# Block 2 of a fused two-block kernel: the transposing turns of the normalised tiles go one tile later, and both first token halves follow the last turn

## The reference, cut to what matters

```python
for l in range(2):
    h = rmsnorm(x, mix_norm_g[l])
    x = x + mixing_layer(h, ...)          # h @ w_in, ..., y @ w_out
    h = rmsnorm(x, ffn_norm_g[l])
    x = x + (silu(h @ w_gate) * (h @ w_up)) @ w_down
return rmsnorm(x, final_norm_g)
```

## Time and profile before

| | |
|---|---|
| time, median of 3 runs | 2886.91 us (2886.65 to 2887.95) |
| time of the profiled execution | 2892.95 us |
| its span | 2891.0 us |
| TensorE matmuls busy | 2699.0 us, 93% |
| TensorE weight loads busy | 2014.6 us, 70% |
| DVE busy | 1096.4 us, 38% |
| ACT busy | 829.0 us, 29% |
| POOL busy | 697.6 us, 24% |
| mean granted TensorE clock | 0.976 |

### The profile page before, as it was taken

How to read it: one execution, slowest core, us unless ns; L and a number is a source line. 1 busy time by engine, 2 the same in 40 slices (tenths; PEclk the granted TensorE clock), 3 DMA queues, 4 the chain that set the end, 5 groups by cost and what they waited for, 6 DMA issues and landing times.

```text
span 2891.0 us, 35167 instructions
## 1 busy us (share of the span) xinstructions
PE 2699.0 (93%) x14496; PEld 2014.6 (70%) x14496; DVE 1096.4 (38%) x1800; ACT 829.0 (29%) x1444; POOL 697.6 (24%) x297
## 2 busy tenths in 40 slices
PE   7999999999989996999999799999999998999998
PEld 4777777786447885444444397888878896988877
DVE  3555555533341124112121488420014697300034
ACT  2433333333333222000000224532222327322122
POOL 2222222220013410000000032233434332343433
PEclk8999999999999997999999999999999999999999
DMA  7111111102012323899999721123222221223221
GB/s 256 52 58 58 58 58 58 36 30 80 27 39 78 127 92 131 351 409 409 409 408 409 293 84 63 59 73 102 88 96 94 73 88 44 74 89 101 89 100 44
DMA packets 212563, 382.38 MB, mean 132 GB/s; under 512 B 10833, under 2 KB 145877, under 8 KB 211413
## 3 DMA queue, kind: packets, MB, share of 16 engines
q1 hardware_dynamic: 211088, 379.06, 36.4%
q10 hardware_dynamic: 1349, 1.51, 0.2%
HBM read 378.44 MB, written 2.10 MB: 132 GB/s over the span
## 4 chain that ended last, share of the span: by engine, by line
PE 69%; DMA 8%; issue 7%; DVE 5%; PEld 5%; ACT 3%; POOL 2%; DVEq 1%; PEldq 0%; SPq 0%; ACTq 0%; POOLq 0%
PE bank L1544 14%; PE bank L1548 13%; PE bank L1549 13%; PE bank L1804 7%; DMA ring<-in_w_up 4%; DMA ring<-in_w_gate 3%; PE bank L1749 2%; PE bank L1692 2%; PEld bank L1352 2%; PE bank L1412 1%; PE bank L1421 1%; PE bank L1598 1%; PE bank L1425 1%; PE bank L1615 1%; PE bank L1318 1%
## 5 line engine op out<-in xcount | busy, mean ns | idle before, releaser
L709 POOL TENSOR_TENSOR w_lo<-ring,w_hi 128x2048 fp32r<-128x2048 f32 x96 | 446.3, 4649 | 1279.0 <-ACT w_hi L721 1279.0
L721 ACT ACTIVATE w_hi<-ring 128x2048 fp32r<-128x2048 f32 (+1 forms) x114 | 215.0, 1886 | 676.4 <-PE bank L1544 676.3
L1544 PE MATMUL bank<-hT_hi,w_hi 128*128 128x512 f32 (+1 forms) x928 | 357.1, 385 | 9.2 <-DVE hT_lo L2595 7.7
L1548 PE MATMUL bank<-hT_lo,w_hi 128*128 128x512 f32 (+1 forms) x928 | 352.8, 380 | 0.0
L1549 PE MATMUL bank<-hT_hi,w_lo 128*128 128x512 f32 (+1 forms) x928 | 349.4, 377 | 0.0
L1804 PE MATMUL bank<-ring,xeT 128*64 128x512 f32 x992 | 225.5, 596 | 30.8 <-DMA ring<-in_w_gate 18.5
L1544 PEld LDWEIGHTS bank<-hT_hi,w_hi 128*128 128x128 f32 x928 | 175.8, 189 | 45.7 <-DVE hT_lo L2595 8.5
L2786 DVE TENSOR_TENSOR ffn_hT<-ffn_sg,bank 128x512 f32<-128x512 f32 x44 | 30.3, 688 | 449.1 <-PE bank L1549 449.1
L1549 PEld LDWEIGHTS bank<-hT_hi,w_lo 128*128 128x128 f32 x928 | 175.5, 189 | 35.7
L1548 PEld LDWEIGHTS bank<-hT_lo,w_hi 128*128 128x128 f32 x928 | 174.9, 189 | 31.8 <-issue 1.0
L1804 PEld LDWEIGHTS bank<-ring,xeT 128*64 128x64 f32 x992 | 77.0, 137 | 155.5 <-issue 152.9
(11 more groups left out here) (492 smaller groups left out, 5058.2 us busy)
## 6 DMA issues: line engine op xcount, KB each, us to landing
ring<-in_w_gate SPq DMA_DIRECT2D x86, 1024.0 KB, 9.1
ring<-in_w_down SPq DMA_DIRECT2D x86, 1024.0 KB, 14.1
ring<-in_w_up SPq DMA_DIRECT2D x82, 1024.0 KB, 14.1
ring<-in_w_in SPq DMA_DIRECT2D x33, 1024.0 KB, 5.2
head_w<-in_w_in SPq DMA_DIRECT2D x32, 512.0 KB, 5.3
mod_w<-in_w_mod SPq DMA_DIRECT2D x8, 2048.0 KB, 8.5
ring<-in_w_out SPq DMA_DIRECT2D x12, 1024.0 KB, 4.8
ring<-in_w_mod SPq DMA_DIRECT2D x8, 1024.0 KB, 16.4
```

The lines of the kernel that those rows point to most:

```text
L709: pool.tensor_tensor(w_lo[m % 2][:], raw[m % RAW][:], w_hi[m % 2][:].bitcast(F32), ALU.subtract).then_inc(lo_ready, 1)
L721: return act.activation(dst, src, ACT.Copy)
L1544: first = mm(dst, a[0], b[0], start=start, stop=False)
L1548: mm(dst, a[0], b[1], start=False, stop=False)
```

## The change

Each turn is made one tile later. TensorE's order becomes: tile 0, tile 1, tile 2, turn 0, tile 3, turn 1, turn 2, turn 3, early half 0, early half 1, late halves. ACT's becomes sum 0, sum 1, sum 2, hi 0, sum 3, hi 1, split of the next chunk, hi 2, hi 3. DVE's becomes x 0, diag 0, x 1, diag 1, x 2, take 0, diag 2, lo 0, x 3, take 1, diag 3, lo 1, take 2, lo 2, take 3, lo 3. It is made at n = 1, 2 and 3.

```diff
--- before.py
+++ after.py
@@ -1083,10 +1083,12 @@
 
             def normed_tiles(n, chunk):
                 tile_sum(n, 0)
-                for t in range(1, TT):
+                tile_sum(n, 1)
+                for t in range(2, TT):
                     tile_sum(n, t)
-                    tile_hi(n, t - 1)
+                    tile_hi(n, t - 2)
                 split(chunk)
+                tile_hi(n, TT - 2)
                 tile_hi(n, TT - 1)
 
             def split_hid(j):
@@ -2067,12 +2069,13 @@
                         if c >= 2:
                             pe.wait_ge(sem("out2_added"), l * 16 + (c - 2) * TT + t + 1)
                         tokens2(bank[c % 2 * 4 + t][:, 0:256], t, y2T, m, before=t == 0).then_inc(sem("x_sum_done"), 1)
-                        if c == 3 and t:
-                            turn_tile(l * 2 + 1, t - 1, free_parts=t == 3)
+                        if c == 3 and t >= 2:
+                            turn_tile(l * 2 + 1, t - 2, free_parts=t == 3)
                     m += 1
-                first_gate(l, m, 0)
+                turn_tile(l * 2 + 1, 2)
                 turn_tile(l * 2 + 1, 3)
-                first_gate(l, m, 1)
+                for b in range(2):
+                    first_gate(l, m, b)
                 tiles_ready(l * 2 + 1, TT)
                 for j in range(FB // 2):
                     for s in range(2):
@@ -2097,12 +2100,13 @@
                                            before=t + hf + b == 0)
                         if j == FB // 2 - 1:
                             last.then_inc(sem("x_sum_done"), 1)
-                            if t and l + 1 < LAYERS:
-                                turn_tile(l * 2 + 2, t - 1, free_parts=t == 3)
+                            if t >= 2 and l + 1 < LAYERS:
+                                turn_tile(l * 2 + 2, t - 2, free_parts=t == 3)
                     m += 1
                 if l + 1 < LAYERS:
+                    turn_tile(l * 2 + 2, 2)
+                    turn_tile(l * 2 + 2, 3)
                     first_projection(l + 1, 0)
-                    turn_tile(l * 2 + 2, 3)
 
 
         @block.vector
@@ -2593,6 +2597,16 @@
                     dve.wait_ge(sem("hT_hi_ready"), n * KD + 2 * t + hf + 1)
                     ks, ts_ = slice(4 * hf, 4 * hf + 4), slice(t * P, (t + 1) * P)
                     tt(hT_lo[:, ks, ts_], h_tmp[:, hf], hT_hi[:, ks, ts_].bitcast(F32), ALU.subtract).then_inc(sem("hT_lo_ready"), 1)
+
+            def last_turns(n):
+
+                take_tile(n, 1)
+                make_diag(n, 3)
+                tile_lo(n, 1)
+                take_tile(n, 2)
+                tile_lo(n, 2)
+                take_tile(n, 3)
+                tile_lo(n, 3)
 
             def moe_scaled(t):
                 dve.wait_ge(sem("moe_rms"), t + 1)
@@ -2766,13 +2780,14 @@
                 n = l * 2 + 1
                 out_tile(3, 0)
                 make_diag(n, 0)
-                for t in range(1, TT):
-                    out_tile(3, t)
-                    take_tile(n, t - 1)
-                    make_diag(n, t)
-                    tile_lo(n, t - 1)
-                take_tile(n, 3)
-                tile_lo(n, 3)
+                out_tile(3, 1)
+                make_diag(n, 1)
+                out_tile(3, 2)
+                take_tile(n, 0)
+                make_diag(n, 2)
+                tile_lo(n, 0)
+                out_tile(3, 3)
+                last_turns(n)
 
                 def hid_lo(j):
 
@@ -2790,13 +2805,14 @@
                     n = l * 2 + 2
                     ffn_tile(0)
                     make_diag(n, 0)
-                    for t in range(1, TT):
-                        ffn_tile(t)
-                        take_tile(n, t - 1)
-                        make_diag(n, t)
-                        tile_lo(n, t - 1)
-                    take_tile(n, 3)
-                    tile_lo(n, 3)
+                    ffn_tile(1)
+                    make_diag(n, 1)
+                    ffn_tile(2)
+                    take_tile(n, 0)
+                    make_diag(n, 2)
+                    tile_lo(n, 0)
+                    ffn_tile(3)
+                    last_turns(n)
 
             def last_scaled(t):
                 dve.wait_ge(sem("rms_ready"), (2 * LAYERS + 2) * TT + t + 1)
```

## The result

The changed kernel takes 2893.09 us (median of 20 runs, 2888.97 to 2898.41) and the kernel before 2889.35 us (median of 20, 2885.19 to 2893.35), both measured side by side. The ratio is 1.0014, 95% interval 1.0008 to 1.0020, so +4.0 us with an interval of +2.3 to +5.8 (the medians by themselves are 3.7 us apart). On the median on which the forecast was made (2886.91) that is 2890.9; forecast were 2891.1 and +4.2 us. The span of its profiled execution is 2891.3 us, 0.3 more than before: one execution of each says nothing about a difference of this size, as both scatter by 4 us and more.

The account below looks back on a forecast made before the run. TensorE, busy 93% of the span, was taken as the bound, with under 10 us of waits reachable. Schedule -0.2 + 1.2 - 0.2 plus clock 2 x 1.7 gave +4.2 us, so 2891.1 us, range 2885.0 to 2895.0.

Parts of the forecast that it names:

- The bound: At n = 1 and 2, late halves' start comes from w_hi, w_lo and the delayed hT_lo, not TensorE: 1906.19, 2284.18.
- the held pair: Two DVE hT_lo operations blocked while POOL's w_lo runs, ending about 1.14 us after it.
- The new price of 2.8 us: Before the late halves: take(3), hi(3), lo(3) now follow the delayed hT_lo of tile 2, 2.8 us.
- How much earlier split starts: ScalarE's split 3.0 us earlier at n = 1 and 3, 1.6 at n = 2; late start -0.2 and +1.2 us.
- The sum of the schedule: Late-start changes at n = 1, 2, 3 without clock effects: -0.2 + 1.2 - 0.2, giving +0.8 us.
- The clock: TensorE's clock falls behind new 2.9 us gaps at n = 1 and 3, costing 1.7 us each.
- No hold: Rival: at the three sites lo(2) runs beside or before w_lo; -10.1 us, time 2876.8; chance 0.08.
- Long fall: Rival: n = 1 and 3 each lose 3.4 us of clock; +7.6, 2894.5; chance 0.22, including equally slow schedules.

Follow-up runs that it names:

- the version with n = 2 only: New order at n = 2 alone, old order at n = 1 and 3, against the kernel before: 0.0 us (-2.6 to +2.3).
- the parts: Two runs against the kernel before: new order at n = 1 and 3 only, +3.8 us; new order at n = 2 only, 0.0 us.

## Why the prediction was right

**The bound.** The late halves start where ScalarE's split and the held pair put them. Right, at both kinds of site: TensorE starts 0.06 and 0.05 us behind the end of the last hT_lo (1903.12 and 2285.40).

**The new price of 2.8 us.** Measured 1903.18 - 1900.35 = 2.83. Right; that hi(2) behind split can only come under a running w_lo was right as well.

**How much earlier split starts.** Forecast 3.0 us at n = 1; relative to diag 0 it came at 11.11 instead of 14.39 us, so 3.3, as two TensorE tiles and turns took a little less than I had taken (turn 1 starts 7.9 us behind diag 0, forecast 8.1). Late start -0.5 for -0.2 us. At n = 2 forecast +1.2, measured +1.16; the gap before turn 3 forecast 2.1, measured 2.09. The gap behind it, forecast 3.4 us, was 1.56, as the fall at turn 3 had filled it; without that fall, in the version with n = 2 only, it is 3.17. The sum of the schedule, forecast +0.8, is +0.15.

**The clock.** Forecast 2 x 1.7 = 3.4 us from the two gaps of 2.9 us. The gaps were 2.6 us. That TensorE's idling is the cause is shown: with the gaps filled and nothing else moved the loss is gone, and the parts put it at n = 1 and 3. The size was a little off: a fall takes 1.7 us of full clock, but the stretch grows by 1.53. What I had not right is that it comes each time: behind six gaps of this length in three profiles it fell four times. By this count the odd sites cost 2 x 4/6 x 1.53 = 2.0 us. Against it stands what I had left out of the sum at n = 2: the fall at turn 3 is covered and takes the place of the old one behind the late gap, which had cost 1.4 us (236.59 less 235.16).

So the places that I named give +0.8 us (0.15 + 2.0 - 1.4), up to +2.2 where turn 3 has no fall, and the measured +4.0 is more. From diag 0 at n = 1 to the down projection of layer 1 the two profiles of the changed kernel are 4.5 and 4.3 us longer than that of the kernel before. Only 1.5 us of this is a fall behind a late gap of an odd site; 1.6 is a fall behind the unchanged ffn_lo gap of layer 0, which came in both and not in the one of before; and 2.7 and 2.4 us are a low clock near 2437 us, inside the attention of layer 1 (worked out from diag 0 at n = 2 to that at n = 3, 239.00 and 238.71 us, less 235.16 and the 1.16 of the schedule; in the profile of before it isn't there). Other profiles say little on whether the change brings that last one: it is in four of the eight with the new order at n = 2 and in one of the five with the old. So the mechanism of the sum was right, and that the total came within 0.2 us of the forecast is luck: a schedule 0.6 us better, falls that come less often and cost less, and a loss of clock elsewhere that I had not reckoned with. Where that comes from stays open.

**The rivals.** "No hold" was rightly given little: it takes moving the split, and then pays 6.6 us, not 10, since at n = 2 the weight chunk becomes the wait. "Long fall" did not occur: no late gap of an odd site was followed by more than one fall of 1.5 us.

## What to carry to other kernels

When a step is moved ahead in one queue, look at what it starts elsewhere: here a copy on ScalarE starts an operation of 4.6 us on POOL, which holds DVE's until it ends, and where that copy stands among the small steps decides more than the order of TensorE's work. Put the start of such an operation behind the last short DVE step that TensorE waits for, or cut it in parts. And don't count gaps of TensorE by their sum alone: at n = 1 and 3 one gap of 2.6 us cost more than two of 1.2 and 1.6 us, because the clock can fall behind it. Whoever fills a gap with unused matmuls must see that they start with it and end before it, or they cost what they save.

## What the runs showed of the hardware

A DVE operation with both inputs in SBUF waits for the POOL instruction that is running, not for POOL's queue: with w_lo cut in four, the pair that took 5.17 us took 2.96, and POOL in turn was held by DVE (a part that came behind a running subtraction of DVE took 1.74 us, the others 1.30). The Trainium skill, SBUF — State Buffer, section "SBUF: two separate sides", has it that the one which comes second is blocked for the whole instruction of the first; these rows agree with it, in both directions. DVE's product of a PSUM tile with gains ran its usual 0.69 us under a w_lo.

Whether the clock falls behind a gap of TensorE varied between executions of the same kernel: never behind four gaps of 1.6 us at n = 1 and 3 in the old order, 15 of 22 times behind 2.01 us, 3 of 5 behind 2.1 us before turn 3, 4 of 6 behind 2.6 us, 2 of 2 behind the old 2.46 us at n = 2, and once behind 3.17 us; neither behind 1.99 nor behind 2.21 us, the waits for the second weight chunk, once each. One fall costs 1.5 us where nothing covers it (behind the ffn_lo gap 1.6), and nothing where TensorE has to wait anyway (turn 3 at n = 2). The runs of one kernel scatter by 4 to 9 us, and their time follows the run's mean clock.
